# Two panels of the convolution's input projection as seven products instead of eight, and a new order of the seven products everywhere

## What is computed

```python
def short_conv_mixer(h, w_in, conv_w, w_out):
    z = h @ w_in
    gate_b, gate_c, u = jnp.split(z, 3, axis=-1)
    g = gate_c * u
    y = lax.conv_general_dilated(g, conv_w[:, None, :].astype(g.dtype), ...)   # causal, depthwise, width 3
    return (gate_b * y) @ w_out

def sq_relu_mlp(h, w_up, w_down):
    return jnp.square(jax.nn.relu(h @ w_up)) @ w_down
```

## Time and profile before

| | before |
|---|---|
| median of 3 runs | 1629.88 us (1629.73 to 1630.76) |
| profiled execution, its own time | 1630.15 us |
| its span, first to last instruction | 1628.4 us |
| TensorE busy | 1598.7 us, 98% |
| DVE, ACT, POOL busy | 1016.4, 725.8, 271.0 us |
| mean granted TensorE clock | 0.998 of full |

### The profile page before, as it was taken

The page is one execution under the profiler, slowest core; times in us unless marked ns, Lnnn a source line. Parts: engine busy times, 40 slices in busy tenths (PEclk is TensorE's granted clock), DMA queues, the critical chain, the costliest instruction groups (busy, mean ns, idle before and its releaser), DMA issues.

```text
span 1628.4 us, 29172 instructions
## 1 busy us (share of the span) xinstructions
PE 1598.7 (98%) x12203; PEld 1417.2 (87%) x12203; DVE 1016.4 (62%) x1416; ACT 725.8 (45%) x1144; POOL 271.0 (17%) x222
## 2 busy tenths in 40 slices
PE   8999999999999999999999999999999999989998
PEld 7998677899999999999887898888887788667896
DVE  6534666388666666555557867677756547856544
ACT  5533554465444444331235544444445445675323
POOL 1002212132222222110004222222212000000200
PEclk9999999999999999999999999999999999999999
DMA  6231030123332222232232333222256676001001
GB/s 197 78 78 31 22 84 10 54 78 130 104 104 89 94 84 99 84 99 93 88 104 78 130 104 104 96 90 100 97 103 99 118 96 89 19 1 62 28 28 52
DMA packets 122689, 134.29 MB, mean 82 GB/s; under 512 B 18877, under 2 KB 99508, under 8 KB 122564
## 3 DMA queue, kind: packets, MB, share of 16 engines
q1 hardware_dynamic: 122362, 132.44, 29.7%
q10 hardware_dynamic: 202, 0.06, 0.0%
HBM read 126.13 MB, written 2.10 MB: 79 GB/s over the span
## 4 chain that ended last, share of the span: by engine, by line
PE 91%; DVE 4%; ACT 2%; issue 1%; DMA 1%; SPq 1%; ACTq 0%; DVEq 0%
PE ps L483 30%; PE ps L1703 22%; PE ps L1650 17%; PE ps L2699 2%; PE ps L829 2%; PE ps L1674 2%; PE ps L812 2%; PE ps L939 1%; PE ps L1220 1%; PE ps L2427 1%; PE ps L837 1%; PE ps L3224 1%; PE ps L2871 1%; PE ps L2850 1%; PE ps L2866 1%
## 5 line engine op out<-in xcount | busy, mean ns | idle before, releaser
L453 ACT ACTIVATE w_hi<-raw 128x1024 fp32r<-128x1024 f32 (+2 forms) x171 | 179.4, 1051 | 400.4 <-PE ps L483 249.4
L483 PE MATMUL ps<-x_hi,w_hi 128*128 128x512 f32 (+4 forms) x872 | 245.8, 333 | 0.5 <-DVE x_lo L503 0.4
L483 PE MATMUL ps<-x_lo,w_hi 128*128 128x512 f32 (+4 forms) x872 | 239.7, 326 | 0.0
L483 PE MATMUL ps<-x_hi,w_lo 128*128 128x512 f32 (+4 forms) x872 | 239.1, 325 | 0.0
L460 DVE TENSOR_TENSOR w_lo<-raw,w_hi 128x1024 fp32r<-128x1024 f32 (+2 forms) x171 | 206.5, 1222 | 45.1 <-ACT w_hi L453 45.1
L1703 PE MATMUL ps<-a_hi,w_hi 128*128 128x258 f32 (+1 forms) x768 | 204.2, 320 | 0.3 <-DVE h L1887 0.3
L1703 PE MATMUL ps<-a_hi,w_lo 128*128 128x258 f32 (+1 forms) x768 | 204.1, 320 | 0.0
L1703 PE MATMUL ps<-a_lo,w_hi 128*128 128x258 f32 (+1 forms) x768 | 204.0, 320 | 0.0
L483 PEld LDWEIGHTS ps<-x_hi,w_hi 128*128 128x128 f32 (+2 forms) x872 | 145.4, 187 | 19.2 <-issue 3.1
L483 PEld LDWEIGHTS ps<-x_lo,w_hi 128*128 128x128 f32 (+2 forms) x872 | 144.6, 186 | 16.4 <-issue 2.2
L483 PEld LDWEIGHTS ps<-x_hi,w_lo 128*128 128x128 f32 (+2 forms) x872 | 144.6, 187 | 14.7
(11 more groups left out here) (489 smaller groups left out, 3343.2 us busy)
## 6 DMA issues: line engine op xcount, KB each, us to landing
raw<-in_w_mlp_up SPq DMA_DIRECT2D x32, 1024.0 KB, 5.3
raw<-in_w_mlp_down SPq DMA_DIRECT2D x32, 1024.0 KB, 5.0
raw<-in_w_in SPq DMA_DIRECT2D x16, 1024.0 KB, 9.6
raw<-in_w_in_conv SPq DMA_DIRECT2D x12, 1024.0 KB, 5.0
raw<-in_w_in_attn SPq DMA_DIRECT2D x8, 1024.0 KB, 5.2
raw<-in_w_out_attn SPq DMA_DIRECT2D x4, 1024.0 KB, 5.0
raw<-in_w_out_conv SPq DMA_DIRECT2D x4, 1024.0 KB, 4.9
raw<-in_w_out SPq DMA_DIRECT2D x4, 1024.0 KB, 5.8
```

The source lines that it names most:

```text
L453: act.activation(split_tile(w_hi, t), raw_tile(t), ACT.Copy).then_inc(w_hi_ok, 1)
L483: ins = pe.matmul(tile_banks(t)[0:m, b, 0:c], w[:, k, :], x[:, k, x0:x0 + c], start=(k == order[0] and n == 0), stop=(k == order[-1] and n ...
```

## The change

Groups i = 2 and 3 of the convolution's projection keep their two C tiles, and their u panel is made of seven products (`FAST` lists all panels done so). The mixing for them is spread over the first eight tiles: one group of mixing begins at each even tile. POOL builds the sums of these two panels after the norm. The loops over the groups on TensorE, ACT and DVE are unrolled. The same code serves the MLPs, and there the order of the seven products changes from 1, 5, 7, 2, 6, 3, 4 to 1, 7, 6, 2, 5, 4, 3. Product 1 is copied into the bank of product 2, where product 2 is added by TensorE, and product 5 and 3 are added on top of 1 and 6 in bank 0, so that one addition falls away and the two halves of the first tile are scaled straight out of PSUM. Lines in the listing are those of the profile before; in the changed file they move by 9 to 80.

```diff
+        cm_hi, cm_lo = [at(n, a_off + i * 16 * HW * 4, [P, 4, 4, HW], F32R) for i, n in enumerate(("cm_hi", "cm_lo"))]
+        s7, s6 = [at(n, t_off + 1056 * i, [P, HW]) for i, n in enumerate(("s7", "s6"))]
...
+        def sums_read(sp, p):
+
+            for n, (layer, u) in enumerate(FAST):
+                if tiles[up_tile(layer, u)][0] == p - 2:
+                    sp.wait_ge(summed, 4 * n + 4)
...
-        ORDER = (1, 5, 7, 2, 6, 3, 4)
+        ORDER = (1, 7, 6, 2, 5, 4, 3)
         X_ROW = {5: 0, 6: 1, 7: 2, 4: 3}
-        P_BANK = {1: 0, 6: 0, 2: 1, 7: 2, 4: 2, 5: 3, 3: 3}
+        P_BANK = {1: 0, 6: 0, 5: 0, 3: 0, 2: 1, 7: 2, 4: 2}
...
+        CONV, FIRST_FAST = 2, (PLAIN, PLAIN, 2)
+        NTH = (0, NS + 2, NS)
+        FAST = [(0, u) for u in range(PLAIN, NU)] + [(CONV, u) for u in range(2, 4)] + [(1, u) for u in range(PLAIN, NU)]
...
+                if not first:
+                    pe.wait_ge(evicted, up_tile(layer, u - 1) + 2)
+                elif layer == CONV:
+                    pe.wait_ge(evicted, T_CONV)
+                    pe.wait_ge(scale_ok, nm.n + 1)
+                else:
                     pe.wait_ge(evicted, MLP_T0[layer] + 2)
...
+            if m == 7:
                 pe.wait_ge(p_lo, 2 * n + 1)
                 if first:
-                    pe.wait_ge(xs["lo"], 4 * layer + 4)
+                    pe.wait_ge(xs["lo"], 4 * nm.n)
                 else:
-                    pe.wait_ge(added, 3 * n)
-            if m == 7 and not first:
-                pe.wait_ge(evicted, up_tile(layer, u - 1) + 2)
-            if m == 2 and not first:
-                pe.wait_ge(evicted, up_tile(layer, u - 1) + 1)
+                    pe.wait_ge(added, 2 * n)
             if m == 6:
                 pe.wait_ge(copied, 3 * n + 1)
                 pe.wait_ge(p_lo, 2 * n + 2)
-            if m == 3:
-                pe.wait_ge(added, 3 * n + 1)
+            if m == 5:
+                pe.wait_ge(copied, 3 * n + 3)
             if m == 4:
                 pe.wait_ge(w_lo_ok, t + 2)
                 pe.wait_ge(copied, 3 * n + 2)
...
-            m, dst = ((1, s1), (7, s7), (6, s6))[which]
+            m, dst = ((1, ps[:, fast_bank(layer, 2), :]), (7, s7), (6, s6))[which]
...
+            if which == 0 and u > FIRST_FAST[layer]:
+                act.wait_ge(evicted, up_tile(layer, u - 1) + 1)
+            if which and n:
+                act.wait_ge(added, 2 * n - 2 + which)
+            act.activation(dst[:, 0:hw], ps[:, fast_bank(layer, m), 0:hw], ACT.Copy).then_inc(copied, 1)
...
+                copy_act(act, nm, layer, 2, 0)
                 square_act(act, nm, layer, 1, 1)
...
-                add("75")
                 add("11")
                 add("22")
+                add("21")
+                scale_dve(dve, nm, layer, u)
                 add("12")
...
-            for j in range(4):
-                dense_tile(pe, T_CONV + j, xh, xl, NW, k_ready=hooks.get(j))
-            with pe.Fori(1, 4) as i:
-                for j in range(4):
-                    dense_tile(pe, T_CONV + j, xh, xl, NW, 4 * i)
+            for i in range(4):
+                for j in range(4 if i < 2 else 2):
+                    dense_tile(pe, T_CONV + 4 * i + j, xh, xl, NW, k_ready=hooks.get(4 * i + j))
+                if i > 1:
+                    for m in ORDER:
+                        product_pe(pe, norm2, CONV, i, m)
...
+            for t in range(8):
+                if t == 0:
+                    act.wait_ge(mm_done, T_CONV)
+                if t % 2 == 0:
+                    mix_made(act, norm2, t // 2)
+                split_hi(act, T_CONV + t + 2)
+                if t == 0:
                     norm_scale(act, norm2)
-            with act.Fori(1, 4) as i:
-                for j in range(4):
-                    split_hi(act, T_CONV + j + 2, 4 * i)
+                if t % 2 == 0:
+                    mix_hi(act, norm2, t // 2)
+            for i in range(2, 4):
+                for part in (0, 2, 3, 1):
+                    prep_act(act, CONV, i, part)
+                t = T_CONV + 4 * i + 4
+                split_hi(act, t, free=t - 3)
+                split_hi(act, t + 1, free=t - 2)
+                for which in range(3):
+                    copy_act(act, norm2, CONV, i, which)
...
+        def conv_taps(dve, i, x):
+
+            j, c, n = 2 + x, 2 * i + x, 2 * i + (x if i < 2 else 1 - x)
+            y = gated[:, c, 0:SEQ]
+            dve.tensor_tensor(lat[:, j, 0:NW], lat[:, j, 0:NW], lat[:, x, 0:NW], ALU.mult).then_inc(cv["g"], 1)
+            dve.wait_ge(cv["g"], n + 1)
+            dve.tensor_scalar(y, lat[:, j, 2:2 + SEQ], col("conv_w", c), None, ALU.mult).then_inc(cv["taps"], 1)
+            for r in (1, 2):
+                dve.wait_ge(cv["taps"], 3 * n + r)
+                dve.scalar_tensor_tensor(y, lat[:, j, 2 + r:2 + r + SEQ], col("conv_w", KC * r + c), y, ALU.mult, ALU.add).then_inc(cv["taps"], 1)
+
         def conv_dve(dve):
...
+            for t in range(8):
+                i, j = t // 4, t % 4
+                if j == 0:
+                    mix_dve(dve, norm2, t // 2)
+                if t == 0:
+                    dve.wait_ge(scale_ok, norm2.n + 1)
+                if i and j < 2:
+                    dve.wait_ge(cv["taps"], 3 * j + 3)
+                conv_evict(dve, i, j)
+                split_lo(dve, T_CONV + t + 2)
+                if j == 2:
+                    mix_dve(dve, norm2, t // 2)
+                if t % 2 == 0:
+                    mix_lo(dve, norm2, t // 2)
+                if j >= 2:
+                    dve.wait_ge(evicted, T_CONV + t + 1)
+                    conv_taps(dve, i, j - 2)
+            for i in range(2, 4):
+                dve.wait_ge(cv["taps"], 6 * i)
+                prep_dve(dve, CONV, i, 0)
+                conv_evict(dve, i, 0)
+                prep_dve(dve, CONV, i, 2)
+                prep_dve(dve, CONV, i, 3)
+                conv_evict(dve, i, 1)
+                prep_dve(dve, CONV, i, 1)
+                split_lo(dve, T_CONV + 4 * i + 4)
+                split_lo(dve, T_CONV + 4 * i + 5)
+                conv_products(dve, i, "11")
+                conv_products(dve, i, "22")
+                conv_products(dve, i, "21")
+                dve.wait_ge(evicted, T_CONV + 4 * i + 2)
+                dve.wait_ge(scaled, nth_up(CONV, i) + 1)
+                conv_products(dve, i, "12")
+                conv_taps(dve, i, 1)
+                dve.wait_ge(evicted, T_CONV + 4 * i + 4)
+                conv_taps(dve, i, 0)
...
+            for u in range(2, 4):
+                for which in range(4):
+                    sums_pool(pool, CONV, u, which)
```

More of the change, by code:

```diff
@@ L1510, in prep_act @@
             if n:
-                before = (layer, u - 1) if u > PLAIN else (0, NU - 1)
-                act.wait_ge(product, max(product_at(*before, m) for m in PART_READERS[part]))
+                act.wait_ge(product, 7 * (n - 1) + max(ORDER.index(m) for m in PART_READERS[part]) + 1)
             dst, src = weight_part(layer, u, part, sw_hi)
@@ L1641, in product_pe @@
                 pe.wait_ge(copied, 3 * n + 2)
+            if m == 3:
+                pe.wait_ge(added, 2 * n + 1)
             for k in range(4):
@@ L1792, in add_products @@
         def add_products(dve, nm, layer, u, what):
-            n, t, hw = nth_up(layer, u), up_tile(layer, u), nm.width // 2
-            b1, b2, b3 = [ps[:, b, 0:hw] for b in (1, 2, 3)]
-            if what == "75":
-                dve.wait_ge(copied, 3 * n + 2)
-                dve.tensor_tensor(s75[:, 0:hw], s7[:, 0:hw], b3, ALU.add).then_inc(added, 1)
+            n, hw, f = nth_up(layer, u), nm.width // 2, nm.first
+            b0, b1, b2 = [ps[:, b, 0:hw] for b in range(3)]
+            read = FF // P * layer + 2 * u
@@ L1799, in add_products @@
             if what == "11":
                 dve.wait_ge(product, product_at(layer, u, 2))
[L1801 to L1803 removed]
+                dve.wait_ge(a_lo_ok, read)
+                dve.scalar_tensor_tensor(tmp[:, 0, hw:2 * hw], b1, 0.0, scale_bc[:, f + hw:f + 2 * hw], ALU.max, ALU.mult).then_inc(evicted, 1)
@@ L1809, in add_products @@
             if what == "12":
                 dve.wait_ge(product, product_at(layer, u, 3))
-                dve.tensor_tensor(tmp[:, 0, 0:hw], s6[:, 0:hw], b3, ALU.add).then_inc(added, 1)
-            if what == "21":
-                dve.wait_ge(product, product_at(layer, u, 4))
-                dve.tensor_tensor(tmp[:, 1, hw:2 * hw], s6[:, 0:hw], b2, ALU.add).then_inc(evicted, 1)
-        def scale_dve(dve, nm, layer, u, tile):
-            n, t, w = nth_up(layer, u), up_tile(layer, u), nm.width
-            dve.wait_ge(added, 3 * n + (2 if tile else 3))
-            dve.wait_ge(evicted, t + tile + 1)
-            dve.scalar_tensor_tensor(tmp[:, tile, 0:w], tmp[:, tile, 0:w], 0.0, scale_bc[:, nm.first:],
-                                     ALU.min if tile else ALU.max, ALU.mult).then_inc(scaled, 1)
```

(7 more changed lines are left out.)

154 lines of the change are left out of this document (74 added, 80 removed).

## The result

The changed kernel takes 1634.78 us (median of 18 runs, 1630.23 to 1638.71), the kernel before in its company 1629.97 (18 runs, 1627.61 to 1634.2). The ratio is 1.0028, with a 95% interval of 1.002 to 1.0036: slower by 4.8 us, where 2.3 were forecast. The stated range was 1628.5 to 1634.7: the median stands 0.1 above its upper end, and the ratio, put on the 1629.88 of the forecast, gives 1634.4, just inside it. By means it is 1634.70 against 1630.31, 4.4 us. The profiled execution took 1634.76.

What follows compares the result with a forecast made beforehand. TensorE's matmuls bound the kernel, unless it is made to wait. Terms -2.9 - 0.5 + 4.0 + 1.7 = +2.3 us on the profiled 1630.15 gave 1632.4, or 1632.2 as median; range 1628.5 to 1634.7.

Steps and rivals of the forecast that it cites:

- 24 matmuls, -2.9: Convolution: two panels with 84 matmuls instead of 96, 24 x 0.120 = 2.9 us less.
- The chain on DVE's list: Convolution: DVE's instruction times summed tile by tile; without POOL the split for tile 9 would be 0.39 us early.
- the rival of the taps' gaps: Convolution: gaps inside taps stay, each set 0.43 us longer, 1.3 us more in all, 1633.5 us; chance 19%.
- POOL's sums against the fourth mixing, 4 x 1.09: Convolution, after tile 7's split: four mixing instructions each lose 1.09 us to POOL's sums, 4.4 us in all.
- The upper bound: Fourth mixing: every instruction waits for a whole sum, 4 x 1.30 = 5.2 us, giving a TensorE wait of 4.8.
- The wait, 4.0: Convolution: TensorE waits 4.0 us before tile 9 for its split; bounds 2.3 and 4.8.
- The clock, "I take one", 1.7: Behind the wait at tile 9: one 3.4 us stretch at half clock, costing 1.7 us; bounds none and two.
- a second stretch: TensorE's clock in the convolution: idle time spread over two half-clock stretches, 1.7 us more, 1633.9 us; chance 5%.
- The second MLP's first panel, -0.5: First such panel of the second MLP: TensorE's wait for `h` shortened, 0.5 us gained; bounds 0 and 0.6.
- the order "at nothing": 28 MLP panels: new waits from the product order covered by about 1 us spare; nothing in all but one panel.
- The rival of slow MLPs: MLPs: spare time eaten by POOL's sums or ACT's queue, 28 x 0.2 = 5.6 us more, 1635 and above; chance 8%.
- The hidden case: Convolution: POOL's sums miss DVE's mixing, tile 9's split on time or under 1 us late, 1626.5 to 1627.5; chance 12%.

Runs made afterwards that it cites:

- experiment 2: Changed kernel with POOL's four sums of group 2 replaced by clears of the same tiles: 1626.94 us, ratio 0.9985 to the kernel before.
- Experiment 3: Kernel before with only the new order of the seven products in both MLPs, convolution as before: 1630.05 us, ratio 0.9998.
- experiment 1: Changed kernel with the fourth mixing moved behind the split for tile 7: 1626.99 us, ratio 0.9986 to the kernel before.
- experiment 4: Changed kernel with tile 6's taps moved behind the split for tile 9, fourth mixing left in place: 1629.7 us, ratio 0.9993 to the kernel before.
- 8: Changed kernel with fourth mixing behind the split for tile 7 and tile 6's taps behind that for tile 9: 1625.61 us, ratio 0.9978.

## Why the prediction was right or wrong

The direction and the mechanism of the wait were right: slower than before by a wait ahead of tile 9, made by POOL's sums. The chances were less sure of it: 57% for a change under 0.2% either way, 37% for slower; it came out at 0.28% slower. The size was too small, +2.3 for +4.8, and what the sum lacked is a term for falls of the clock outside the convolution. By its own steps:

- *24 matmuls, -2.9.* Right: 12203 to 12179, at the same pace.
- *The chain on DVE's list.* Right to 0.2 us from the split for tile 4 to that for tile 9. Tiles 5 to 8 see no wait. Inside a set of taps the gaps are 0.03 (748.59 to 749.11 for 0.49), so the rival of the taps' gaps is false.
- *POOL's sums against the fourth mixing, 4 x 1.09.* The first instruction lost 1.12, the others 1.00 each: 4.1 for 4.4. The upper bound, by which each would lose a whole sum, 1.29 to 1.5, came out 0.3 to 0.5 an instruction too high. The Trainium skill (SBUF — State Buffer, "Who interferes with whom") has the one that comes second blocked until the first is done. The trace agrees with that: the sum of 742.55 ends at 743.84, and the mixing instruction that began 0.15 later, 0.43 long by itself, ends at 744.12. What was too high is the reckoning of a whole sum for each, since the sum had already begun. That it is the reading which collides is shown by experiment 2.
- *The wait, 4.0.* TensorE lost 4.0 in three traces, but in part by luck. The forecast's 4.0 was the gap alone, which came out at 3.74, since the contention was 0.26 smaller than taken (4.1 for 4.36); the 0.26 lost at the restart had no term and happened to make it up.
- *The clock, "I take one", 1.7.* About right as an average, and not as described. At half clock two matmuls start every 0.43 us (753.47 to 753.90), 0.215 each for 0.120, so that a stretch costs 0.44 of its length, 1.5 us and not 1.7. In the three traces of the changed kernel the clock behind the wait cost 1.3, 1.4 and 2.5, on average 1.7. What I gave 5% as a rival of its own, a second stretch, is a share of the executions of the very same kernel. The Trainium skill (TensorE: Matmul & The Clock Gate, "Part 1") has the clock go to half after an idle window and back after a busy one, and the prediction took from it that a wait which reaches into a second window brings two low stretches. The traces so far agree: 6.83 us are two stretches of 3.41, and in all three traces that have them the clock fell 0.8 us or more before TensorE restarted.
- *The second MLP's first panel, -0.5, and the order "at nothing".* Experiment 3 measured 0.27 gained at that panel and 0.4 given back at about 0.03 a panel, and further small shifts; together 0.2 us in the trace and a ratio of 0.9998. The term should have been near zero. The rival of slow MLPs is false, too: no wait lies there.
- *Falls of the clock elsewhere.* The forecast had no term for them, as if they were the same before and after, and this is where most of the missing time lies. In the two profiled executions the terms above make -2.9 - 0.2 + 4.0 + 1.3 = +2.2. The rest are falls that only one of the two has, priced by the traces of experiment 1 and of the changed kernel: +4.7 for the 10.24 us at 1564, -1.6 for the missing fall at 269, -0.5 for the missing one at 1508. The sum is +4.8; the spans differ by 4.5.

The runs can be checked in the same way, since each has its mean granted clock on record, and one minus that clock, times two, times the time is what it spent at half clock. The mean clock is 0.9958 over the 18 runs of the changed kernel, 0.9962 over the 12 timed again, and 0.9981 to 0.9987 for the kernel before in its three later companies. That is 13.6 and 12.5 us at half clock in a run against 4.4 to 6.2. The 12 have 7.6 us more than the 27 runs beside them, which at 0.44 is 3.3 us; for the 18, whose own company has no clock on record, the 35 runs of the next company give 3.3 too. With it the sum is -2.9 - 0.2 + 4.0 + 3.3 = +4.2, and the means say 4.4 and 4.0. Of the 3.3 about 1.7 lie behind the wait, by the three traces, and the rest, about 1.6, elsewhere. With so few traces this division is uncertain by some 0.5 us. Whether the change makes falls elsewhere more frequent is not shown: the one of 10.24 us stands in two of the three traces of the changed kernel and in that of experiment 4, and in none of the other nine.

The hidden case, given 12%, is what experiments 1, 2 and 8 made of the kernel: 1627.0, 1626.9 and 1625.6, against the 1626.5 to 1627.5 worked out for it.
